# Attention of a hybrid decoder: a few VectorE steps each moved one item back in a hand-written order

## What is computed

```python
def block(b):                                   # 128 queries
    sc = jnp.einsum('bhgqd,bhcd->bhgqc', qb, kc)
    pc = masked_softmax(sc, mc)                 # compressed keys
    o_cmp = jnp.einsum('bhgqc,bhcd->bhgqd', pc.astype(vc.dtype), vc)
    ...
    ps = masked_softmax(ss, pos_s <= t[:, None])    # selected blocks
    o_slc = ...
    pwin = masked_softmax(jnp.einsum('bhgqd,bhkd->bhgqk', qb, kwb), mw)
    o_win = ...
    return gb[..., 0:1] * o_cmp + gb[..., 1:2] * o_slc + gb[..., 2:3] * o_win
...
mix = jnp.concatenate([y_ret, y_nsa], axis=-1) @ w_out[l]
x = x + rms_norm(mix, ln_mix_post[l])
```

## Time and profile before

| | us |
|---|---|
| median of 3 runs | 1379.64 (1379.24 to 1380.26) |
| the profiled execution, its own time | 1378.21 |
| its span | 1376.4 |
| TensorE matmuls busy | 1351.3 (98%) |
| VectorE / ScalarE / GpSimd busy | 725.5 / 603.2 / 698.8 |

### The profile page before, as it was taken

How to read it: one execution, slowest core, us unless ns; L and a number is a source line. 1 busy time by engine, 2 the same in 40 slices (tenths; PEclk the granted TensorE clock), 3 DMA queues, 4 the chain that set the end, 5 groups by cost and what they waited for, 6 DMA issues and landing times.

```text
span 1376.4 us, 17693 instructions
## 1 busy us (share of the span) xinstructions
PE 1351.3 (98%) x6904; PEld 1113.3 (81%) x6904; DVE 725.5 (53%) x908; ACT 603.2 (44%) x1039; POOL 698.8 (51%) x544
## 2 busy tenths in 40 slices
PE   8999999999999999999999999999999999999998
PEld 5889876778888888888888888767798888888886
DVE  5506658745554544654463075677355554556443
ACT  5233577745433333423441336676463333334222
POOL 2544677744544444544465456776544444445441
PEclk9999999999999999999999999999999999999999
DMA  5433320031432333333233334101233333333331
GB/s 205 138 99 108 119 81 16 1 123 62 118 97 92 102 98 92 97 103 92 62 123 102 116 100 134 34 15 43 81 98 102 105 94 92 104 96 92 98 102 61
DMA packets 34883, 127.19 MB, mean 92 GB/s; under 512 B 3952, under 2 KB 4464, under 8 KB 34416
## 3 DMA queue, kind: packets, MB, share of 16 engines
q1 hardware_dynamic: 34656, 125.53, 29.5%
q10 hardware_dynamic: 144, 0.52, 0.1%
HBM read 123.94 MB, written 2.10 MB: 92 GB/s over the span
## 4 chain that ended last, share of the span: by engine, by line
PE 87%; ACT 5%; DVE 4%; issue 2%; POOL 1%; DMA 0%; DVEq 0%; POOLq 0%; ACTq 0%; SPq 0%
PE bank L1755 33%; PE bank L1408 17%; PE bank L1787 17%; PE bank L1424 5%; PE bank L1652 3%; PE bank L1690 2%; ACT E L825 1%; PE bank L1713 1%; PE bank L1512 1%; PE bank L1714 1%; DVE pt_l L945 1%; PE bank L1619 1%; PE bank L1598 1%; PE bank L1376 1%; DVE s_bias L1209 1%
## 5 line engine op out<-in xcount | busy, mean ns | idle before, releaser
L550 POOL TENSOR_TENSOR w_lo<-raw,w_hi 128x1024 fp32r<-128x1024 f32 x216 | 519.8, 2412 | 469.7 <-ACT w_hi L650 469.3
L650 ACT ACTIVATE w_hi<-raw 128x1024 fp32r<-128x1024 f32 x220 | 231.0, 1055 | 240.8 <-DMA raw<-wstream 240.5
L1755 PE MATMUL bank<-act_hi,w_hi 128*128 128x512 f32 (+1 forms) x768 | 286.0, 372 | 0.6 <-DVE act_lo L945 0.6
L1755 PE MATMUL bank<-act_hi,w_lo 128*128 128x512 f32 (+1 forms) x768 | 285.2, 371 | 0.0
L1755 PE MATMUL bank<-act_lo,w_hi 128*128 128x512 f32 (+1 forms) x768 | 285.2, 371 | 0.0
L904 ACT ACTIVATE cv<-bank,par 128x512 f32<-128x512 f32 x88 | 68.4, 778 | 286.0 <-PE bank L1755 286.0
L1337 DVE SCALAR_TENSOR_TENSOR cv<-bank,par,cv 128x511 f32<-128x511 f32 x88 | 66.0, 749 | 225.2 <-ACT cv L904 225.2
L1755 PEld LDWEIGHTS bank<-act_hi,w_hi 128*128 128x128 f32 x768 | 144.6, 188 | 26.9 <-DVE act_lo L945 1.6
L1755 PEld LDWEIGHTS bank<-act_lo,w_hi 128*128 128x128 f32 x768 | 144.7, 188 | 25.0
L1755 PEld LDWEIGHTS bank<-act_hi,w_lo 128*128 128x128 f32 x768 | 144.6, 188 | 24.8
L1408 PE MATMUL bank<-w_hi,act_hi 128*128 128x512 f32 (+1 forms) x384 | 144.5, 376 | 0.6 <-DVE w_lo L945 0.5
(11 more groups left out here) (178 smaller groups left out, 2195.2 us busy)
## 6 DMA issues: line engine op xcount, KB each, us to landing
raw<-wstream SPq DMA_DIRECT2D x220, 512.0 KB, 3.6
g_all<-gains SPq DMA_DIRECT2D x2, 2048.0 KB, 7.2
x_out<-x SPq DMA_DIRECT2D x8, 256.0 KB, 2.0
x<-x_in SPq DMA_DIRECT2D x3, 512.0 KB, 9.1
const<-consts SPq DMA_DIRECT2D x1, 1030.0 KB, 13.7
x<-x_in SPq DMA_DIRECT2D x2, 256.0 KB, 5.2
g_all<-gains ACTq DMA_DIRECT2D x1, 512.0 KB, 5.1
par<-pars SPq DMA_DIRECT2D x2, 235.0 KB, 3.6
```

The costliest lines, as they stand in the source:

```text
L550: nc.gpsimd.tensor_tensor(w_lo[:, s, :], raw_slot(s), r32(w_hi[:, s, :]), ALU.subtract)\
L650: nc.scalar.activation(w_hi[:, s, :], raw_slot(s), ACT.Copy).then_inc(hi_ready, 1)
L1755: last = mm(bank[:, b, first:end], a, v, start=(k == 0 and n == 0), stop=(k == KD - 1 and n == 2), skip_group_check=True)
```

## The change

Four things, each in the order alone; no instruction is added or taken out. The jobs of the narrow units 6 and 7 move from items 7 and 10 to 8 and 11, and with them all that hangs on a job's item. out_sum, out_round and out_rest of v = 0 to 6 move one item back (OUT_LAG 4 in place of 3); out_first stays at last + 3, and v = 7 is left as it was. The subtraction of the compressed minimum is split off compressed_first as compressed_lowered: for group 0 it stays in its place, for group 1 it comes at item 25 in place of 24, and the group's exponential and four statistics steps follow one item later. The output projection's blocks (0, 0) and (0, 1) move from items 27 and 28 to 28 and 29.

```diff
+        OUT_LAG = lambda v: 3 if v == T * NKV - 1 else 4
-        WO_AT = {27: [(0, 0)], 28: [(0, 1)], 31: [(3, 0)], 32: [(3, 1)], 38: [(2, 0)], 39: [(2, 1)], 40: [(3, 2)],
+        WO_AT = {28: [(0, 0)], 29: [(0, 1)], 31: [(3, 0)], 32: [(3, 1)], 38: [(2, 0)], 39: [(2, 1)], 40: [(3, 2)],
                  41: [(3, 3)], 42: [(1, 0)], 43: [(1, 1)], 44: [(2, 2)], 47: [(2, 3)]}
-        UNIT_SCORES = {4: (3, 4), 5: (5, 6), 6: (7,), 7: (10,), 8: (12, 13, 14, 16), 9: (17, 18, 19, 20),
+        UNIT_SCORES = {4: (3, 4), 5: (5, 6), 6: (8,), 7: (11,), 8: (12, 13, 14, 16), 9: (17, 18, 19, 20),
...
-                    if k - 4 in LAST_OF_V.values():
-                        out_rest(ITEMS[k - 4][1])
+                    for v, last in LAST_OF_V.items():
+                        if k == last + OUT_LAG(v) + 1:
+                            out_rest(v)
...
-                        if k == CMP_AT[g] + 1:
+                        if k == CMP_AT[g] + g + 1:
                             act.wait_ge(c_step, upto(c_step, l, 7 * g + 3))
...
-                    if k - 3 in LAST_OF_V.values():
-                        out_first(ITEMS[k - 3][1])
-                    if k - 4 in LAST_OF_V.values():
-                        out_round(ITEMS[k - 4][1])
+                    for v, last in LAST_OF_V.items():
+                        if k == last + 3:
+                            out_first(v)
+                        if k == last + OUT_LAG(v) + 1:
+                            out_round(v)
...
+                def compressed_lowered(g):
+                    at, b = 7 * g, CMP_BANK[g]
+                    rows = bank[:, b, :].rearrange("p (r c) -> p r c", c=NCP)
+                    stat = c_stat[:, g * 16:g * 16 + 16]
                     dve.wait_ge(c_step, upto(c_step, l, at + 2))
                     nc.vector.tensor_tensor(cE[:, g], rows, stat.unsqueeze(2).broadcast_to([P, 16, NCP]),
                                             ALU.subtract).then_inc(c_step, 1)
...
                     if k == CMP_AT[1]:
                         compressed_first(1)
+                    if k == CMP_AT[1] + 1:
+                        compressed_lowered(1)
                     for g in range(NKV):
-                        compressed_step(g, k - CMP_AT[g])
+                        compressed_step(g, k - CMP_AT[g] - g)
...
-                    if k - 3 in LAST_OF_V.values():
-                        out_sum(ITEMS[k - 3][1])
+                    for v, last in LAST_OF_V.items():
+                        if k == last + OUT_LAG(v):
+                            out_sum(v)
```

More of the change, by code:

```diff
@@ L1258, in _ @@
                         compressed_first(0)
+                        compressed_lowered(0)
                 def p_rest(k):
```

## The result

The changed kernel takes 1387.23 us in the median of six runs, against 1379.44 us before: a ratio of 1.0055, 95% interval 1.0044 to 1.0066. One of the six took 4741.33 us, for a reason that no run shows: it is left out of the ratio, but that median contains it, and the median of the other five is 1385.60 (1385.52 to 1389.56, mean 1387.0). Measured again later, with another six runs, the kernel took 1386.44 (ratio 1.0045, 1.0030 to 1.0060). The mean of all eleven ordinary executions is 1386.8, against 1380.0 for before. So it is slower by 6 to 8 us. The forecast was 1383.8 with a range up to 1386.2; sign and main place were right, the size was too small. The miss is narrow: 1385.60 lies inside the range, 1386.44 and the mean lie just above it. The profiled execution of after took 1385.52 us with a span of 1383.6, 7.2 us more than the span of before.

What follows compares the result with a forecast made beforehand. TensorE, busy 1351.3 of 1376.4 us, was taken as the bound. Per layer 2.03 from the k=44 wait plus about 0 from the rest, 4.1 for two layers, on 1379.64 gave about 1383.8 us, range 1381.0 to 1386.2.

Steps and rivals of the forecast that it cites:

- Part 1: Jobs of units 6 and 7 moved: gap before transposes 10 stays 1.62 us, transposes 13 about 0.7 late.
- Part 2: Output sums one item later: transposes 14 come 0.46 us early, 21 0.62 early; taken as -0.6 a layer.
- Part 3: VectorE's clump at k=24: transposes 27 and 28 wait, lead becomes a 0.2 lag; +0.65 us a layer, 0 to +1.4.
- Part 4: At k=44 wo_half_0(2, 2) waits for act_lo of v=5: +2.03 us a layer, bounds 1.7 to 2.4.
- A: The forecast itself: 1.7 to 2.4 us a layer from the k=44 wait, -0.4 to +0.3 from the rest; chance 0.62.
- B: The k=44 wait comes, but the later output sums' lead survives k=25 to 29: 1382.4, down to 1381.0 us; chance 0.19.
- D: More waits: later out_round delays several pt_h in the clumps, further 0.8 to 1.5 us a layer, 1385.4 to 1387; chance 0.08.
- rival E: TensorE's clock falls in a stall of 2 us, costing 2 us a stall: 1388 us; chance 0.03.

Runs made afterwards that it cites:

- the fill: First retention tile transposed four times over at k=8: in the changed kernel 1384.13 us (ratio 1.0028), in the kernel before 1379.29 us (ratio 0.9995).
- the fastest version: Changed kernel with outputs v=2 and v=5 at their old items, block (2, 2) at item 45 and fourfold transposes at k=8: 1376.26 us, ratio 0.9977.

## Why the prediction went wrong, point by point

**The order of the work was read well.** The start of the transposes against before, layer 0, from the timelines (less the shift that was there at k=0). The middle column is the second measurement, whose layer 0 ran at full clock:

| transposes | predicted | full clock | profiled execution of after |
|---|---|---|---|
| 13 | +0.7 | +0.60 | +2.22 |
| 14 | -0.46 | -0.63 | +0.98 |
| 15 | -0.69 | -0.64 | +0.98 |
| 16 | -0.08 | -0.05 | +1.58 |
| 17 | -0.39 | -0.36 | +1.27 |
| 21 | -0.62 | -0.64 | +0.99 |
| 30 | +0.2 | -0.19 | +1.42 |
| 44 | about 0 | -0.43 | +1.20 |
| 45 | +2.0 | +1.76 | +3.41 |

The last column is the middle one plus 1.6 throughout: the fall comes before transposes 12.

**Part 1** held: the gap before transposes 10 was 1.55 (1.62 before), and 13 came 0.60 late. **Part 2** held: -0.64 at 21, with -0.6 taken.

**Part 3** had the size a little high and the place wrong. I let transposes 27 wait for pt_l of k=25. In fact the product of item 24 waits for out_sum(2), 1.06 us: they share an output bank, a dependence that I had not looked for. I followed the moved step along VectorE's queue, and not to everyone who needs the bank that it frees. The lag of 0.2 at transposes 30 was a lead of 0.19, and at 44 a lead of 0.43. So parts 1 to 3 are worth -0.43 a layer, taken as 0, inside my -1.0 to +0.6. It was an error in the direction opposite to the miss.

**Part 4** was right in mechanism and chain and 0.2 small: transposes 45 to 47 stand 2.2 us later against 44 (1.76 + 0.43), for 2.03 predicted and a bound of 2.4. Together parts 1 to 4 come to +1.8 a layer, 3.6 for two; the forecast was 4.1. Every wait in the sum, then, is within half a microsecond of what was said, and would have given some 1383.2. (The forecast's own sum is 1383.7, not 1383.8, and the bounds of rivals A, B and D differ from their terms by up to 0.3 us, which changes nothing here.)

**The step that failed** is the clock. The sum has no term for it, and rival E, which has, was given a chance of 0.03; in the profiled execution of after it costs 3.2 us beside the 3.6 of the order. Three readings were wrong. First, "no fall at k=10" rested on one execution of before, and on its window with the gap (217 to 221). That window could not have shown a fall: in after, too, the stretch with the gap stands at 1.00, and the fall comes behind it. The stretch behind it in before, 222 to 226, is at 1.00 as well, but this execution was a quiet one. It had a mean clock of 0.999, and the executions of before average 0.9963: 46 of the 79 have 0.997 or less, where the two profiles without any fall in attention (before, and before with the fill) have 0.999 and 0.998. The kernels with v=5 and with v=2 late alone, which at k=10 still run in the order of before, fall behind that very gap in layer 1. Second, E tied a fall to the new stall of 2 us. Such falls exist (from 976.5 with the jobs back, from 294.4 with the fill), but those of after came at the old gap, which the change leaves at 1.55 us and follows with one of 0.61 before transposes 11. Third, the fall has no fixed price. E took 2 us from the earlier trace rows and after paid 1.6; in the order of before the same fall costs 0.90, because the gap before transposes 14, which the change closes, makes good most of the rest.

The sentence of the Trainium skill quoted in E ("TensorE: Matmul & The Clock Gate", section "What's actually happening") names the lower level, and the runs agree: 0.50 from 248 to 252 with v=5 late alone. That the array must be idle for it is not what they show. Ahead of the falls of after TensorE was half busy, and before those from 246.7 (v=5 late alone) and 924.3 (the fastest version) the timeline shows no gap in the 10 us before.

**The account of the profiled execution.** Span 1383.6 less 1376.4 is 7.2. Before attention 0.24; the wait at k=44 less what parts 1 to 3 win, twice 1.8, 3.6; two falls of the clock, 3.2; 0.2 is left over. After has a low stretch near the start too (the clock is 0.87 from 8 to 12 us, 1.00 in before), which may be the 0.24.

**The account of the means.** Over all executions after is 6.8 us above before (1386.8 against 1380.0); 3.6 of it is in the order of the work, and the remaining 3.2 would have to be clock. The profile of before, at 0.999, took 1378.2, so before loses about 1.8 us to falls in the mean; after would be at 1381.8 without any and loses 5.0. By the prices above (0.9 in before, 1.6 in after) that would be about two falls an execution in before and three in after. This is an estimate from few profiles: that a fall is dearer in the changed order is shown in single layers, that there are more of them only by the mean clock (0.9945 over eleven executions against 0.9963). A straight line through the executions fits with it: 0.001 of mean clock goes with 0.52 us in before and with 0.84 in after. The mean clock is itself no price, because it also counts stretches in which TensorE has nothing to do, like the end of before (clock 0.56 from 1373 us on, TensorE not busy at all).

**What else stays open.** When a fall comes and why it stays away in one execution. Of the 19 low stretches in attention, 13 begin behind the gap at k=10 or 11, four at the end of one of the new waits of 1.8 to 1.9 us or up to 1.3 us behind it, and two (from 246.7 and 924.3) behind none. No run tells why the changed kernel has more of them than before. Several waits seem to have a share: the mean clock goes from 0.9945 to 0.9962 with the fill, to 0.9954 with v=5 put back, to 0.9965 with block (2, 2) at item 45 and to 0.9964 with the jobs back, but with 5 to 10 executions each these cannot be told from one another. So the kernel with the jobs back, which should be 2 us slower than after by its order, was 1.1 faster in the mean (1385.7 against 1386.8); its mean clock is higher, and one of the two falls in its profile cost only 0.4. With the jobs' shift the order wins 1.0 a layer, and little of it arrived in the median in the versions without the fill.

## What to carry to other kernels

A step moved back in one queue has to be followed to every reader of what it frees, the accumulator bank and the counter that several outputs share among them; here each of the two that were overlooked or uncovered cost 2 us a layer when moved alone. Where TensorE is 98% busy and single gaps are about 1.5 us, look at the mean clock of every execution, not only at the one profiled: a stretch at clock 1.00 in one execution does not say that the kernel keeps it. A small gap further on is not only waste: it can make good a part of a fall, as the one before transposes 14 did, and closing it can win less than a profile without a fall shows. A gap that can't be closed can be filled with redundant transposes: with twelve a layer the longest gap went from 1.55 to 0.25 at a cost of about 0.1 us a layer. The version that had the fill, left the two tight outputs where they were and moved block (2, 2) was 3.2 us faster than before.

## What was not expected of the hardware

The clock falls behind gaps as short as 1.55 and 0.61 us in a row, to a mean of 0.57 in the 4 us that follow, and also behind a single one of 1.64; four 128-column transposes take 1.11 us instead of 0.66. What a fall at k=10 costs ran from 0.4 to 1.6 us for a low stretch as long as those of after, and from 1.4 (v=2 late alone) to 2.7 (v=5 put back) for one twice as long. The same kernel with the same gaps falls in one execution and not in the next: layer 0 took the 4.10 us step in one profile and 2.49 in the other. The mean clock of the kernel before ran from 0.991 to 0.999 over 79 executions.
